# 64 tokens by fetched rows, and the up-projection of a PEER layer as unsplit fp32 products

## The reference, cut to what matters

```python
def peer_ffn(xn, w_peer_q, sub_keys, expert_u, expert_v):
    qh = (xt @ w_peer_q).reshape(T, PEER_HEADS, 2, PEER_HALF)
    s = jnp.einsum('thpd,hpnd->thpn', qh, sub_keys)
    sv, si = lax.top_k(s, PEER_TOPK)
    ...
    best, pick = lax.top_k(cand, PEER_TOPK)
    expert_idx = jnp.take_along_axis(cand_idx, pick, axis=-1)
    gates = jax.nn.softmax(best, axis=-1)
    ...
        hval = jnp.einsum('cd,chkd->chk', xc, expert_u[ic])
        a = gc * jax.nn.gelu(hval, approximate=False)
        return jnp.einsum('chk,chkd->cd', a, expert_v[ic])
```

## Time and profile before

| | us |
|---|---|
| median of 3 runs | 1311.26 (1310.68 to 1311.98) |
| the profiled execution, its own time | 1311.49 |
| its span, first to last instruction | 1309.7 |
| busy: PE / PEld | 1294.8 / 1199.0 |
| busy: DVE / ACT / POOL | 1068.7 / 820.4 / 220.7 |
| all before the first U unit | 619.5 |
| U units (128) | 368.5 |
| dense V units (120) | 288.0 |
| the rest | 33.7 |

### The profile page before, as it was taken

How to read it: one execution, slowest core, us unless ns; L and a number is a source line. 1 busy time by engine, 2 the same in 40 slices (tenths; PEclk the granted TensorE clock), 3 DMA queues, 4 the chain that set the end, 5 groups by cost and what they waited for, 6 DMA issues and landing times.

```text
span 1309.7 us, 21763 instructions
## 1 busy us (share of the span) xinstructions
PE 1294.8 (99%) x8061; PEld 1199.0 (92%) x8061; DVE 1068.7 (82%) x1974; ACT 820.4 (63%) x1601; POOL 220.7 (17%) x163
## 2 busy tenths in 40 slices
PE   8999999999999999999999999999999999999998
PEld 6998888888889888888999999999999999999996
DVE  6968776666678656769999989999999989998985
ACT  6886465555556555454666888888765555555553
POOL 3001130000000000000100021110234336544410
PEclk9999999999999999999999999999999999999999
DMA  6533366555445344654666666556799999999972
GB/s 228 178 124 126 113 226 193 191 190 185 160 159 177 129 145 150 235 200 150 211 207 222 207 214 207 196 204 214 270 346 323 367 356 346 363 366 352 342 278 89
DMA packets 82784, 292.74 MB, mean 224 GB/s; under 512 B 10397, under 2 KB 11053, under 8 KB 82422
## 3 DMA queue, kind: packets, MB, share of 16 engines
q1 hardware_dynamic: 68182, 239.65, 52.8%
q0 software_dynamic: 14496, 51.69, 10.9%
HBM read 288.95 MB, written 2.34 MB: 222 GB/s over the span
## 4 chain that ended last, share of the span: by engine, by line
PE 86%; DVE 7%; ACT 3%; issue 2%; DMA 1%; SPq 0%; POOL 0%; POOLq 0%; DVEq 0%; ACTq 0%
PE bank L2408 84%; DVE wl L665 2%; PE bank L2506 1%; ACT wh L1745 1%; DMA raw<-in_wts 1%; PE bank L2494 1%; DVE oi L1580 1%; DVE rows L1603 1%; DVE gates L1635 1%; DVE oj L1576 0%; ACT oi L2328 0%; ACT oi L2332 0%; DVE gates L1588 0%; ACT kdz L1751 0%; DVE St L855 0%
## 5 line engine op out<-in xcount | busy, mean ns | idle before, releaser
L2408 PE MATMUL bank<-hTb,wh 128*128 128x416 f32 (+3 forms) x2768 | 823.8, 363 | 1.5 <-DVE wl L665 1.3
L2408 PE MATMUL bank<-hTb,wl 128*128 128x208 f32 (+2 forms) x2584 | 651.8, 264 | 0.0
L665 DVE TENSOR_TENSOR wl<-raw,wh 128x1024 fp32r<-128x1024 f32 x429 | 523.1, 1226 | 128.7 <-ACT wh L1745 126.9
L1745 ACT ACTIVATE wh<-raw 128x1024 fp32r<-128x1024 f32 x429 | 449.0, 1055 | 203.4 <-PE bank L2408 132.4
L2408 PEld LDWEIGHTS bank<-hTb,wh 128*128 128x128 f32 (+1 forms) x2768 | 504.3, 188 | 22.2 <-issue 2.9
L2408 PEld LDWEIGHTS bank<-hTb,wl 128*128 128x128 f32 (+1 forms) x2584 | 491.5, 190 | 4.8
L2408 PE MATMUL bank<-wh,hTb 128*128 128x512 f32 (+2 forms) x552 | 175.6, 400 | 1.7 <-DVE hTb L699 1.7
L2408 PEld LDWEIGHTS bank<-wh,hTb 128*128 128x128 f32 (+1 forms) x552 | 102.4, 187 | 24.6 <-DVE wl L665 1.8
L645 POOL DMA_INDIRECT rows<-in_v_rows,pick x48 | 97.4, 2029 | 98.3 <-DVE acc L1614 85.7
L645 POOL DMA_INDIRECT rows<-in_u_rows,pick x48 | 70.6, 1471 | 229.7 <-DVE dots L1603 227.5
L2408 PE MATMUL bank<-wl,hTb 128*128 128x512 f32 (+2 forms) x276 | 100.7, 390 | 0.0
(11 more groups left out here) (429 smaller groups left out, 1396.1 us busy)
## 6 DMA issues: line engine op xcount, KB each, us to landing
raw<-in_wts SPq DMA_DIRECT2D x441, 512.0 KB
x<-in_x SPq DMA_DIRECT2D x4, 256.0 KB, 6.9
sk<-in_sk SPq DMA_DIRECT2D x1, 1024.0 KB, 7.3
spill<-x SPq DMA_DIRECT2D x1, 1024.0 KB
x<-spill SPq DMA_DIRECT2D x4, 256.0 KB
rows<-in_u_rows,pick POOLq DMA_INDIRECT x48
rows<-in_v_rows,pick POOLq DMA_INDIRECT x48
gb<-in_g_ffn SPq DMA_DIRECT2D x1, 512.0 KB
```

Source lines behind the costliest of these rows:

```text
L665: e.tensor_tensor(b[:, :], raw[u % RAW][:, :], a[:, :].bitcast(F), ALU.subtract).then_inc(S("lo"), 1)
L1745: e.activation(parts_of(u)[0][:, :], raw[u % RAW][:, :], ACT.Copy).then_inc(S("hi"), 1)
L2408: return e.matmul(o, l, r, start=first, stop=last, skip_group_check=True)
```

## The change

Six things are changed together.

- **Tokens.** MORE goes from 16 to 32, so 64 tokens go by fetched rows (64 slots of U and 64 of V) and TN = 192 are dense.
- **Unsplit units.** `WHOLE` names the U units that are computed as plain fp32 products straight from `raw`: all units before GATED = 85 (37 before the gates and 48 during them), and behind it every second one (n even, 21 of 43). Their activations are `xt`, the sum of both halves of `hTb`, written once by POOL into the place of `x` after `x` is spilled. A whole unit is 8 products of 192 columns, has no split on ACT and DVE, no low half, no copy and no sum; gelu reads PSUM directly. SP refills its `raw` only when PE is done with it.
- **Split units** remain 22 U units behind the gates, and all V units.
- **Stages.** NP goes from 50 to 36, NC from 52 to 48. `at_keys` and the exponentials move to earlier units.
- **One-hots.** NB goes from 5 to 3 buffers; DVE makes `oi` for every third group of four tokens, ACT for the others.
- **Slots.** Of the 128 slots 40 are taken at the units from NP + 9 through the gates, one each, 28 at two of every three units behind the gates, and 60 in the V stage. Before, of 96, 28 were taken at U units and 68 in the V stage.

```diff
-NP, NB = 50, 5
+NP, NB = 36, 3
-MORE = 16
+MORE = 32
+WHOLE = tuple(n for n in range(NE) if n < GATED or n % 2 == 0)
...
+        xt = sb("xt", [128, 8, TN], F, XO)
...
         def added(n):
-            return n < SUMMED or n < GATED and n % 2 == 0
+            return n not in WHOLE and (n < SUMMED or n < GATED and n % 2 == 0)
...
-            at = {GATED - 1 - 3 * k: SOON - 1 - k for k in range(SOON)}
-            for n in range(GATED, NE - 2, 2):
-                at[n] = len(at)
+            at = {NP + 9 + k: k for k in range(NC - 8)}
+            for n in range(GATED, NE - 1):
+                if (n - GATED) % 3 < 2:
+                    at[n] = len(at)
...
                     if u >= RAW:
-                        e.wait_ge(S("lo"), u - RAW + 1)
+                        if u - RAW in whole_units:
+                            e.wait_ge(S("done"), u - RAW + 1)
+                        else:
+                            e.wait_ge(S("lo"), nth_split(u - RAW))
...
+            e.wait_ge(S("hT_lo"), 24)
+            e.wait_ge(S("in_end"), 16)
+            e.tensor_tensor(xt[:, :, :], hTh[:, :, 0:TN].bitcast(F), hTl[:, :, 0:TN].bitcast(F),
+                            ALU.add).then_inc(S("hT_lo"), 1)
...
-            at_keys = {20: (0, 0, 0), 21: (0, 0, 1), 23: (0, 1, 0), 25: (0, 1, 1),
-                       36: (1, 0, 0), 37: (1, 0, 1), 38: (1, 1, 0), 39: (1, 1, 1)}
+            at_keys = {15: (0, 0, 0), 16: (0, 0, 1), 17: (0, 1, 0), 18: (0, 1, 1),
+                       27: (1, 0, 0), 28: (1, 0, 1), 29: (1, 1, 0), 30: (1, 1, 1)}
...
-                if n == 41:
+                if n == 32:
...
-                if c % 2 == 0:
+                if on_vector(c):        # c % 3 == 0
...
+            def unit_whole(unit, bank):
+                ...
+                e.wait_ge(S(f"raw{n % RAW}"), 16 * (n // RAW + 1))
+                e.wait_ge(S("hT_lo"), 25)
+                for k in range(8):
+                    t = mm(bank[:, 0:TN], raw[n % RAW][:, two(128, k)], xt[:, k, :], k == 0, k == 7)
+                t.then_inc(S("done"), 1)
```

More of the change, by code:

```diff
@@ L295, in program @@
         M = Area(R0, RE)
-        oj = [M(f"oj{i}", [128, 4, 128]) for i in range(3)] + [sb(f"oj{i}", [128, 4, 128], F, XO + 2048 * (i - 3))
-                                                              for i in (3, 4)]
-        oi = [sb("oi0", [128, 4, 128], F, X0 + 3072)] + [M(f"oi{i}", [128, 4, 128]) for i in (1, 2)] + \
-             [sb(f"oi{i}", [128, 4, 128], F, XO + 2048 * (i - 1)) for i in (3, 4)]
+        xt = sb("xt", [128, 8, TN], F, XO)
+        oj = [M(f"oj{i}", [128, 4, 128]) for i in range(3)]
+        oi = [sb("oi0", [128, 4, 128], F, X0 + 3072)] + [M(f"oi{i}", [128, 4, 128]) for i in (1, 2)]
         GT0 = M.p
@@ L351, in program, with nth_split, split_of @@
         Q0 = nth("T", "w_peer_q_2", 0, 512, 0)
+        U0 = nth("U", ORDER[0])
+        whole_units = tuple(U0 + n for n in WHOLE)
+        def nth_split(u):
+            return u + 1 - sum(w <= u for w in whole_units)
+        def split_of(n):
+            return min(n, NE - 1) + 1 - sum(w <= n for w in WHOLE)
         def parts_of(u):
@@ L389, in nth_sum, with on_vector, nth_on @@
                 return n - 3
-            return 13 + n - nth_added(n)
+            return 12 + split_of(n) + max(0, n - NE + 1) - nth_added(n)
+        def on_vector(c):
+            return c % 3 == 0
+        def nth_on(vector, c):
+            return sum(on_vector(i) == vector for i in range(c + 1))
         def added(n):
-            return n < SUMMED or n < GATED and n % 2 == 0
+            return n not in WHOLE and (n < SUMMED or n < GATED and n % 2 == 0)
         def nth_added(n):
@@ L656, in low @@
                 for u in range(lows[0], min(n + 1, len(units))):
-                    e.wait_ge(S("hi"), u + 1)
+                    if u in whole_units:
+                        continue
+                    e.wait_ge(S("hi"), nth_split(u))
                     if units[u][1] == "w_ple_gate":
@@ L1590, in summed @@
             def summed(n):
+                if n in WHOLE:
+                    return
                 u = us[n % 2][:, :]
@@ L2266, in gelu @@
                     e.wait_ge(S("u_add"), nth_added(n))
-                else:
+                elif n not in WHOLE:
                     e.wait_ge(S("u_sum"), nth_sum("U", n))
@@ L2282, in block_out @@
                 e.wait_ge(S("done"), nth("U", ORDER[n]) + 1)
-                if not added(n):
-                    e.wait_ge(S("gelu"), n - 1)
-                copy((low_half if added(n) else us)[n % 2][:, :], B[2 + n % 4][:, TN:2 * TN]).then_inc(S("u_out"), 1)
+                if n not in WHOLE:
+                    if not added(n):
+                        e.wait_ge(S("gelu"), n - 1)
+                    copy((low_half if added(n) else us)[n % 2][:, :], B[2 + n % 4][:, TN:2 * TN]).then_inc(S("u_out"), 1)
                 high(nth("U", ORDER[n]) + LOOK)
@@ L2320, in one_hots @@
             def one_hots(c):
-                if c % 2 == 0:
+                if on_vector(c):
                     return
@@ L2347, in scalar, with factors @@
                 copy(gates[:, 0:NE - n, two(4, c)], v[:, 0:NE - n, :]).then_inc(S("G_out"), 1)
-            after_dots = {j: n for n, j in slots_taken()[1].items()}[SLOTS - 1] + 1
+            at_u, at_v = slots_taken()
+            after_dots = {j: n + 1 for n, j in at_v.items()}.get(SLOTS - 1, -1)
+            after_dots_u = {j: n + 1 for n, j in at_u.items()}.get(SLOTS - 1, -1)
+            def factors():
+                e.wait_ge(S("used"), used_by(SLOTS - 1))
+                e.activation(factor[:, :], dots[:, :], ACT.Gelu).then_inc(S("used"), 1)
             def high_of(n):
@@ L2366, in scalar @@
                     high_of(n - NE + 6)
+                if n == after_dots_u:
+                    factors()
             gelu(NE - 1)
@@ L2381, in scalar @@
                 if n == after_dots:
-                    e.wait_ge(S("used"), used_by(SLOTS - 1))
-                    e.activation(factor[:, :], dots[:, :], ACT.Gelu).then_inc(S("used"), 1)
+                    factors()
                 if n == DENSE:
@@ L2443, in unit_M @@
                         mm(bank[:, 0:width], wl_[:, c], hTh[:, k, 0:width], False, False)
+                t.then_inc(S("done"), 1)
+            def unit_whole(unit, bank):
+                n = nth(*unit)
+                assert n == started[0], (unit, units[started[0]])
+                started[0] += 1
+                e.wait_ge(S(f"raw{n % RAW}"), 16 * (n // RAW + 1))
+                e.wait_ge(S("hT_lo"), 25)
+                for k in range(8):
+                    t = mm(bank[:, 0:TN], raw[n % RAW][:, two(128, k)], xt[:, k, :], k == 0, k == 7)
                 t.then_inc(S("done"), 1)
@@ L3122, in early @@
                     e.wait_ge(S("gelu"), n - 3)
-                unit_M(("U", ORDER[n]), B[2 + n % 4], width=TN)
+                if n in WHOLE:
+                    unit_whole(("U", ORDER[n]), B[2 + n % 4])
+                else:
+                    unit_M(("U", ORDER[n]), B[2 + n % 4], width=TN)
                 if n and added(n - 1):
```

18 lines of the change are left out of this document (9 added, 9 removed).

## The result

The changed kernel takes **1316.3 us** in the median of 8 runs (1311.0 to 1318.0), the kernel before 1311.5 beside it (8 runs, 1310.7 to 1313.7). The ratio is 1.0035, with a 95% interval of 1.0027 to 1.0044: slower by a third of a per cent, where 1305 was forecast and 1315 was the upper end of the range. The profiled execution of the changed kernel took 1317.97 us, the longest of the eight and 1.65 above the median; its span is 1316.2.

What follows compares the result with a forecast made beforehand. PE was taken as the bound, busy 1294.8 of 1309.7 us. From 1311.49: U stages +5.5, V stage -12.8, DMA +1, giving 1305.2; with the median 0.2 below the profiled execution, forecast 1305.0 us, range 1297 to 1315.

Steps and rivals of the forecast that it cites:

- whole unit: U units on PE: plain fp32 products of 192 columns cost 2.61 us a unit, bounds 2.61 to 2.66.
- rival C: U units on PE: a whole unit is dearer, 2.66 us, adding 5.3 us, 1310 in all; chance 0.16.
- unit with gate products: U during the gates: 3.51 us on PE, with DVE and ACT below that per unit, so their cover costs 0.
- k step of a split unit: Split U and V units on PE: 0.300 us falls to 0.287, only the long product gaining; 2.29 us a unit.
- rival B: Split units on PE: no floor, both products shrink with their columns, 0.280 a step, 1297.5 in all; chance 0.14.
- top-k: U before the gates: ends at 714 us, needed by 715.5; 1.5 us of slack, 0 in the sum.
- rival E: Start of the gates: the top-k ends late and PE waits 3 to 4 us, 1308.5; chance 0.09.
- all U stages: U on PE: 374.0 us, +5.5, from prices of whole units, split units and gate products plus 1 us.
- V: V stage on PE: 12.8 us less than 288.00, from 120 x 8 steps each 0.0133 us shorter.
- the one on DMA: Behind the gates 354 GB/s, 97 to 99% of what is there; in V 345, as now; 1 us added.
- rival D: Behind the gates and in V: transfers become the bound; at 335 GB/s they take 394.6 us, 1319; chance 0.13.
- The forecast's own sign: Behind the gates: a DMA share of 0.97 or more, with PE still fully busy there.

Runs made afterwards that it cites:

- two more buffers and the order: Changed kernel with six raw buffers, and at V's start ACT and DVE finish the last gates unit before splitting the third V unit; 1298.0 us, ratio 0.9903.
- the order alone: Changed kernel with its four raw buffers, last gates unit's gelu and product put ahead of the next V units' splits on ACT and DVE; 1318.9 us, ratio 1.0061.
- swapped fetches: Changed kernel where, behind the gates, SP issues the split unit's fetch before the one waiting for a whole unit; four buffers, same bytes; 1310.2 us, ratio 0.9997.
- row fetches left out: Changed kernel with the 28 row fetches behind the gates replaced by tiny ones, so part of the expert sum uses old rows; 1308.0 us, ratio 0.9989.
- order and swap: Changed kernel with four raw buffers, fetches swapped in pairs behind the gates and ACT's and DVE's order changed at V's start; 1308.5 us, ratio 0.9987.

## Why the prediction was wrong

**The prices held.** U without gates, as a group of PE, and the gate products of three neighbouring units, which answer to the earlier trace rows:

```profile
L2450 PE MATMUL bank<-xt,raw 128*128 128x192 f32 x576 | 93.9, 326 | 0.0
...
841.56 1.05 PE L2450 MATMUL bank<-oi,oj 128*128 128x128 f32 x8
845.05 1.05 PE L2450 MATMUL bank<-oi,oj 128*128 128x128 f32 x8
848.54 1.05 PE L2450 MATMUL bank<-oi,oj 128*128 128x128 f32 x8
```

A whole unit is 93.9 / 36 = 2.61 us, as forecast; rival C (2.66) falls. A unit with gate products is 3.49 us (forecast 3.51). A k step of a split unit is 273.0 / 960 = 0.2844 us in V without idle time, between the forecast's 0.287 and rival B's 0.280 (some runs show 0.290, see the last section). The top-k ended at 713.7 us, forecast 714, and PE is idle for 0.2 us of the whole stretch with gates, so rival E didn't come. With early fetches all U stages take 990.03 - 618.55 = 371.5 us (forecast 374.0) and V 273.0 (275.2): the sum of prices was 4.7 us too high. The kernel it describes is the one with more buffers and the new order, at 1298.0 us: 4.7, the 1 us put for DMA and a start of U 0.9 us earlier are nearly all of the 7 us between the two.

**The step that failed** is the one on DMA: "So V asks for nothing new, and the stage behind the gates for 97 to 99% of what is there. I add 1 us." It compared bytes with a rate. It didn't ask when each fetch can start and when it must have landed. The text had both halves in view, that two fetches are issued together when a whole unit ends, and that a split unit must be ready ahead of its products, and put them into rival D, priced as a rate, but not into the sum. Worked out from rows that were there: 9.8 us from issue to use, less a split of 1.05 + 1.22, is 7.5 us; a pair of fetches and the rows between them are 1.7 MB, which at 354 GB/s is 4.9 us per pair with the next pair already queued. In the kernel before, unit u's buffer came free when unit u-4 was split, at best seven units ahead of PE's use of u (three by LOOK, four by the buffers), 16.8 us by an estimate from 2.40 us a unit, where it is 9.8 now. The late weights cost 114.7 - 105.2 = 9.5 us behind the gates, where 1 was put, and more in V, where nothing was put.

**V** came out at 283.4 us instead of 275.2. At its start (PE, then ACT, then PE again, in order of time), and ACT's wait for weights in the rest of V (1006 to 1282):

```profile
1001.10 0.41 PE L2450 MATMUL bank<-ab,wh 128*128 128x384 f32 x1 [0.58 <-DVE wl L694]
...
1002.55 1.06 ACT L1778 ACTIVATE wh<-raw 128x1024 fp32r<-128x1024 f32 x1 [3.74 <-DMA raw<-in_wts]
...
1005.16 0.36 ACT L2306 ACTIVATE ga<-us 128x192 f32<-128x192 f32 x1 [1.12 <-DVE us L1625]
...
1005.58 0.69 PE L2450 MATMUL bank<-ab,wh 128*128 128x384 f32 x1 [3.12 <-ACT ga L2306]
...
ACT wh L1778 <- DMA raw<-in_wts: 93.3, 68, 3.9
```

ACT waits 3.74 us for the weights of a V unit, the gelu stands behind that, and PE behind the gelu. With two more gaps late in V (0.27 and 1.03 us) that is 5.0 us. Then the granted clock, in windows of 3 us:

```profile
1002.00:1005.00 3.00, 0.46 (x4) 0.22 (x2) 1.37 (x2) 1.49 (x3) 0.04 (x1) 0.81 0.97 345
1005.00:1008.00 3.00, 2.42 (x9) 2.42 (x10) 2.44 (x7) 1.81 (x4) 0.00 (x0) 0.50 1.01 385
1008.00:1011.00 3.00, 3.00 (x14) 3.00 (x13) 1.75 (x3) 2.06 (x3) 0.00 (x0) 0.55 0.75 279
```

After the gap PE runs at 1.2 GHz until about 1010.5, a step in 0.53 us instead of 0.285: some 2.4 us lost, 3.3 at most (0.16 of the 20.8 us at a clock of 0.84). A third part is in the last section. Five, 2.4 to 3.3 and 1.4 are 9 to 10 of the 10.4 us above 273.0. In the run with two more buffers and the order all of them are gone; in that with the order alone none is. So the gaps and the half clock follow from late weights: at the start of V from the fetch that waits for the last whole unit, later from those of V's own split units, for which ACT waits 93.3 us, where it waited 62.6 before and 1.3 with two more buffers and the order. Whether the later ones are what is left of the delay behind the gates, or four buffers are too few for units of 2.29 us, no run tells apart; with all units split behind the gates they are there too. For the third part no cause was found.

**Rival D** had the sign, a gap on PE that ends with `wl`, and nearly the time, 1319, which is luck. It named the short lead and the two fetches together, but what it priced was another mechanism, "the transfers become the bound", with the engines down to 335 GB/s. They show 328, but because they are asked too late: the share is 0.92, and 356 to 368 GB/s are there for the same bytes with more buffers. The forecast's own sign, a share of 0.97 or more with PE fully busy, was missed on both counts. Here a rate below the sum of bytes over time, at a share of 0.92, was the mark of a late start.

**The ledger**, in spans. Forecast -6.3 us, seen +6.5, a difference of 12.8: behind the gates +9.5 less the 1 put there, V +8.2, U up to the end of the gates 266.9 against 268.8 (-1.9), an earlier start of U (617.65 against 619.50, -1.9; unexplained, but it varies between 617.3 and 619.0 in the other runs), the end -0.1.

What stays open: why single runs of the four-buffer versions lie up to 15 us apart (1311.4 to 1326.6 with the order alone), where the six-buffer ones lie within 3.4. That late fetches are sensitive to small shifts would explain it, but no run was made for it.

## What to carry to other kernels

When an operand goes to the matmul directly and no longer through a split, its buffer is held until the product is done: count for each fetch the time from the event that frees its buffer to the moment when its first reader must begin, and hold that against issue to landing in the trace. A comparison of bytes with GB/s can't see it. Where fetches of two kinds stand in one list, the one whose buffer comes free first goes first and doesn't wait behind the other's buffer, which here cost no buffer and gave 5 to 6 us; and after such a change the mix that was best before is to be tried again, since each shift moves load between engines.

## What the runs showed of the hardware

**The same row of matmuls has two steady prices.** In V each step is one product of 384 and one of 192 columns. The same 1808 records, with two more buffers and with the swapped fetches, PE full in both and the granted clock at 1.00:

```profile
1008.70:1265.50 256.80, 256.80 (x1808) 256.80 (x1807) 230.56 (x286) 148.55 (x229) 104.76 (x55) 1.00 0.96 351
...
1011.70:1273.50 261.80, 261.80 (x1808) 261.80 (x1807) 230.89 (x286) 148.21 (x229) 90.09 (x55) 1.00 0.94 343
```

That is 0.2841 and 0.2896 us a step, 5.0 us over the stage. In either run the price holds for all of this stretch. In the changed kernel it is 0.2845 from 1011 to 1187.8, 0.290 from there to 1260.5, and then 0.2845 again: 73 us at the higher one, 1.4 us. Neither change lies at a gap (the nearest are 0.27 us before 1192.88 and 1.03 us before 1273.96); with all units split behind the gates both changes do (gaps of 1.07 and 0.84 us before 1112.80 and 1227.93), and not every gap changes it. The row fetches left out: 0.290 throughout, at 351 GB/s and a share of 0.96 from 1010 to 1260; order and swap: 0.2845 throughout, at 353 and 0.96. So neither the instructions nor the load of the DMA engines decides it, and what does was not found. The Trainium skill (TensorE: Matmul & The Clock Gate, Back-to-back issue gap) prices an isolated product by its columns, which makes some 0.245 us of this step, an estimate, and says that weight loads and products together set the spacing in a stream; both measured prices are above the estimate. The two prices bound what a single profile can say about changes of some 5 us here.

**A short gap can cost its length again in clock.** The gaps of 0.2 to 1.5 us behind the gates left the granted clock at 1.00; that of 3.12 us, 4 us after one of 0.58, was followed by 5 us near 0.50; one of 2.02 us in the kernel with the order alone by 0.50 from 1003 to 1009, with a first product of 0.64 us in place of 0.41. With two more buffers one of 1.84 us was enough for 0.50 from 994 to 997. With the fetches swapped two of 0.94 and 1.51 us, 2.9 us apart, brought 0.65 from 994 to 997; with one more buffer two of 0.93 and 0.80 us, 2.2 us apart, left it at 1.00.
